# A seventh place for an expert's weights where X was, X kept in the output meanwhile, one buffer for a pair's rows, and the first weights in two loads

## The chip, the cores and the metric

The kernel runs on one core of a Trainium2 chip. Times are device microseconds of one execution. Before the change three runs took 669.09, 669.54 and 670.16 us, so the median is 669.54 us.

The engines of the core: TensorE (PE in the rows; PEld is its weight load), VectorE (DVE), ScalarE (ACT), GpSimd (POOL) and SyncE (SP). SP issues nearly all loads, POOL the indirect gathers and scatters and some stores, ACT the stores of the output. Each engine runs its own list of instructions in order and waits for others at semaphores.

## The reference, cut to what matters

One layer for 640 tokens of 1024 numbers: 512 of a new stream and 8 streams of 16. All is float32.

```
h = RMSNorm(x); z = h @ w_in                       # 3088 columns
x = x + concat(diff_attention(z), gla(z)) @ w_out
h = RMSNorm(x)
group = argmax(h @ w_group); two experts inside the group: top-2 of h @ w_erouter
y = x + sum over the two experts of weight * (silu(h @ w_gate[e]) * (h @ w_up[e])) @ w_down[e]
```

There are 4 groups of 8 experts, so 32 experts. Each has 1024x256 gate, 1024x256 up and 256x1024 down weights: 2048 KB for gate and up together (one load, `egu`) and 1024 KB for down (one load, `edn`). Every expert is loaded whole, 96 MB in all.

## The kernel before, in words

The tokens are 5 tiles of 128. The stages in order: transposes of x and the projection by w_in in six chunks of columns, each in two halves of the inner dimension; linear attention between the chunks; the attention of the prompt; the attention of the streams; w_out and the residual, which leaves its sum in the tile `X` (words 0 to 5K of each partition of a big `arena`); the second norm, the router and tables of which token goes to which slot; then the experts; then the sum.

**The experts.** They run in 16 pairs, 64 slots for each expert, so a pair fills 128 partitions. A pair p takes these steps:

- POOL gathers the pair's rows of the normed input from DRAM into `xs` (line 731). Two buffers. The gather of pair p waits for `xsT_done`: PE must have transposed the rows of pair p-2.
- PE transposes them (line 2225, 8 matmuls), DVE scales them into `xsT` (line 1669), PE multiplies by gate and up (`gate_up`, line 2236, 32 matmuls), ACT and DVE make the hidden values, PE transposes those (line 2244), ACT copies them (line 1066), PE multiplies by down (`down_proj`, line 2256, 16 matmuls).
- ACT copies the two banks to `ysb` (line 1077) and POOL scatters them to DRAM, `ye_dram` (line 719). There are two buffers `ysb`, taken in turn, and ACT waits for the scatter of pair p-2 before it fills one again.

PE's order in the loop is: gate_up(p), down_proj(p-1), transposes of the rows of pair p+1, transposes of the hidden values of pair p. ACT's is: silu(p), `ysb` of pair p-1, hidden values of pair p. POOL's is: gather(p), then scatter(p-4), and so on (`late = 4`).

**The weights.** Six places in the arena (`EPLACE`, `NBUF = 6`) hold an expert each, expert e in place e % 6. The first five load while the stages ahead still run, as soon as each place is free. Place 5 lies on the router's tables and waits for the first two gathers (`gath`, the wait behind line 544). From then on SP loads the gate and up weights of experts 2k+4 and 2k+5 when gate_up of k pairs is done (line 523), and down weights of two experts when down_proj of a pair is done (line 526). All go on one queue, in order.

**The end.** When the last scatter has landed, SP loads the 1280 rows from DRAM in five loads into `yg` (line 586). DVE adds them to `X` with the routing weights (line 1707), and ACT stores the tiles (line 1103). `X` stays in place through all of this.

**The front.** SP loads tile 0 of x, the gains, the first half of the first chunk of weights (`win`, 1024 KB, line 454), then more of x. ACT splits weights into a high part `wH` (line 761), DVE makes the low part `wL` (line 1129), PE transposes tiles of x (line 1720) and multiplies (lines 1734 to 1736).

Of the kernel before, what the change touches and what calls it, by code (L numbers as in the profile page):

```python
# [20 lines left out]
ALU = mybir.AluOpType  # L21
# [3 lines left out]
P = 128  # L25
D = 1024
DC = D // P
# [26 lines left out]
NBUF = 6  # L54
# [18 lines left out]
def build(nc, x, cache_kt, cache_v, state, w_main, w_ga, w_a2b, w_out, cols, k_gain, lam, w_r, b_r,  # L73
          w_gu, w_dn, y_out, k_out, v_out, sp_out, ss_out, hn_dram, ye_dram):
    ctx = ExitStack()
    with ctx:
# [3 lines left out]
        def sem(name):  # L80
            return ctx.enter_context(nc.semaphore(name))
# [137 lines left out]
        EPLACE = [28 * KW, 34 * KW, 40 * KW, 5 * KW, 11 * KW, 17 * KW]  # L219
# [5 lines left out]
        ysb = [at(f"ysb{k}", 23 * KW + k * D, D) for k in range(2)]  # L225
# [4 lines left out]
        YG = [40 * KW, 42 * KW, 44 * KW, 5 * KW, 7 * KW]  # L230
# [66 lines left out]
        ld_small = sem("ld_small")  # L297
        ld_win = [sem(f"ld_win{k}") for k in range(2)]
# [19 lines left out]
        wga_ready = sem("wga_ready")  # L318
# [40 lines left out]
        sp_ready = sem("sp_ready")  # L359
        ss_ready = sem("ss_ready")  # L360
# [8 lines left out]
        vs_ready = sem("vs_ready")  # L369
# [56 lines left out]
        st_y = [sem(f"st_y{k}") for k in range(2)]  # L426
        ysum = sem("ysum")
        st_out = sem("st_out")

# [22 lines left out]
        def _(sp):  # L452
            def w_half(c, k):
                sp.dma_start(win[k][:, :], w_main[c * P:(c + 1) * P, k * HW:(k + 1) * HW]).then_inc(ld_win[k], 16)
# [6 lines left out]
            w_half(0, 0)  # L461
# [38 lines left out]
            sp.wait_ge(ss_ready, 1)  # L500
# [29 lines left out]
            sp.wait_ge(vs_ready, 1)  # L530
# [17 lines left out]

            for k in range(NXS):
                sp.wait_ge(gath[k], 16)  # L550
            gate_up_of(5)
            for e in range(NBUF, NE + 2, 2):
                if e < NE:
                    sp.wait_ge(gu_done, e // 2 - 2)
                    gate_up_of(e)
                    gate_up_of(e + 1)
                if e > NBUF:
                    sp.wait_ge(dn_done, e // 2 - 3)
                    down_of(e - 2)
                down_of(e - 1)  # L560
# [12 lines left out]
            with sp.If(sp.value_load(ovf[0:1, 0:1]) > 0):  # L573
                sp.wait_ge(gu_done, PAIRS)
                sp.wait_ge(dn_done, PAIRS)
                with sp.Fori(1, ROUNDS) as r:
                    with sp.Fori(0, NE // 4) as g:
                        experts(r * 8, g)
                for k in range(2):
                    sp.wait_ge(st_y[k], ROUNDS * (PAIRS // 2) * 16)  # L580

            for k in range(2):
                sp.wait_ge(st_y[k], PAIRS // 2 * 16)
# [9 lines left out]
        def _(pool):  # L593
# [75 lines left out]
            pool.wait_ge(sp_ready, 1)  # L669
            pool.dma_start(sp_out, S).then_inc(st_states, 16)  # L670
            pool.wait_ge(ss_ready, 1)
# [18 lines left out]
            pool.tensor_copy(zVs[:, :], z(C_V, NP)).then_inc(vs_ready, 1)  # L690
# [17 lines left out]
            def pairs(r):  # L708
                first = isinstance(r, int)
                t0 = before(r, 2 * PAIRS, 2 * (PAIRS + 1))  # L710

                def seen():
                    if not first:
                        pool.sem_inc(pool_seen, 1)

                def scatter(p):
                    pool.wait_ge(ysb_ready, r * 2 * PAIRS + 2 * (p + 1))
                    seen()
                    pool.indirect_dma_start(  # L719
                        out=ye_dram, out_offset=bass.IndirectOffsetOnAxis(ap=dst[:, p:p + 1], axis=0),  # L720
                        in_=ysb[p % 2][:, :], in_offset=None, bounds_check=2 * NT * P - 1, oob_is_err=False,
                    ).then_inc(st_y[p % 2], 16)
# [26 lines left out]
        def _(act):  # L749
# [7 lines left out]
            def w_high(c, k):  # L757
                act.wait_ge(ld_win[k], (c + 1) * 16)
                for s in range(4):
                    o = slice(s * 512, (s + 1) * 512)  # L760
                    act.activation(wH[k][:, o], win[k][:, o], ACT.Copy, scale=g1[:, 4 * k + s:4 * k + s + 1]  # L761
                                   ).then_inc(wH_ready, 1)
# [55 lines left out]
            def qT_out(i):  # L818
                act.wait_ge(qT_done, i + 1)
                act.wait_ge(gains_ready, 2)  # L820
                act.activation(qT[:, :, i * P:(i + 1) * P],
                               bank[6 + (NT + i) % 2][:, :].rearrange("p (h t) -> p h t", h=H),
                               ACT.Copy, scale=qg8[:, 0:1]).then_inc(qT_ready, 1)

            for c in range(1, 6):
                for k in range(2):
                    for i in range(NT):
# [52 lines left out]
                        if u == U_QTR:  # L880
                            act.wait_ge(go_done, NT)
                            act.wait_ge(ss_ready, 1)
# [152 lines left out]
            h2_out(0)  # L1035
            std_out(0)
            stream_squares()
            a_high(2)
            h2_out(1)
            std_out(1)  # L1040
# [3 lines left out]
            h2_out(2)  # L1044
            std_out(2)
            a_high(4)
            h2_out(3)
            std_out(3)
            hn_out(2)
            h2_out(4)  # L1050
            std_out(4)
# [36 lines left out]
            with act.If(act.value_load(ovf[0:1, 0:1]) > 0):  # L1088
                with act.Fori(1, ROUNDS) as r:
                    with act.Fori(0, NE // 4) as g:  # L1090
                        for q in range(2):
                            silu(r, 2 * g + q, q)
                            hidden(r, 2 * g + q, q)
                        for q in range(2):
                            act.wait_ge(dn_done, r * PAIRS + 2 * g + q + 1)
                            act.wait_ge(st_y[q], (r * (PAIRS // 2) + g) * 16)
                            for hf in range(2):
                                act.activation(ysb[q][:, hf * 512:(hf + 1) * 512], bank[4 + 2 * q + hf][:, :],
                                               ACT.Copy).then_inc(ysb_ready, 1)
# [7 lines left out]
        def _(dve):  # L1107
# [30 lines left out]
            for i in range(NT):  # L1138
                dve.wait_ge(ld_x[i], 16)
                if i:  # L1140
# [6 lines left out]
                              bc(g1, [P, DC, RANK]), ALU.mult).then_inc(wga_ready, 1)  # L1147
# [64 lines left out]
            def states(i):  # L1212
# [23 lines left out]
                if i == NP - 1:  # L1236
                    dve.nop().then_inc(sp_ready, 1)
# [29 lines left out]
            for c in range(1, 6):  # L1267
                for k in range(2):
                    for i in range(NT):
# [54 lines left out]
                        if u in U_SU:  # L1324
                            stream_states(U_SU.index(u))
                            if u == U_SU[-1]:
                                dve.nop().then_inc(ss_ready, 1)
# [297 lines left out]
            def tables(r):  # L1625
# [11 lines left out]
                else:  # L1637
                    for q in range(2):
                        dve.wait_ge(st_y[q], r * (PAIRS // 2 * 16))
# [62 lines left out]
            for i in range(NT):  # L1702
                dve.wait_ge(ld_x[i], 3 * 16)
# [8 lines left out]
        def _(pe):  # L1712
# [11 lines left out]
            def proj(c, k, i):  # L1724
# [4 lines left out]
                for s in range(DC // 2):  # L1729
# [19 lines left out]
            for i in range(2, NT):  # L1749
                proj(0, 0, i)  # L1750
# [3 lines left out]
            pe.wait_ge(wga_ready, 1)  # L1754
# [310 lines left out]
            def d_pv(b):  # L2065
                pe.wait_ge(d_pt_ready, 2 * b + 2)
                if b == 0:
                    pe.wait_ge(vs_ready, 1)
# [193 lines left out]
            def first_places(p):  # L2262
                return [(2 * p + j) % NBUF for j in range(2)], [2 * p // NBUF + 1] * 2
# [93 lines left out]
```

## Time and profile before

| | us |
|---|---|
| median of 3 runs | 669.54 |
| profiled execution | 669.5 |
| its span in the trace | 667.5 |
| its time outside the span | 2.0 |
| PE busy | 566.3 (85%) |
| DVE busy | 250.8 (38%) |
| ACT busy | 191.8 (29%) |
| POOL busy | 88.7 (13%) |

The profile comes from one execution. Its time, 669.5 us, agrees with the median. The page cuts the span into 40 slices of 16.7 us; the experts fill slices 24 to 39 and the slices before them are bound in turn by PE and by short chains between engines. In the rows, a matmul's busy time is counted whole while matmuls overlap. A DMA has two times: that of its issue on a queue, and the time from its issue to its landing. "DMA share" is the mean over the core's 16 DMA engines.

### The profile page before, as it was taken

What the parts mean: (1) busy time and instruction counts of PE and PEld (TensorE: products, weight loads), DVE (VectorE), ACT (ScalarE), POOL (GpSimd) and SP (SyncE); (2) the same over time, 40 slices, a digit from 0 to 9 for tenths busy, and PEclk for the clock granted to TensorE, in tenths of its full rate; (3) what the DMA queues carried; (4) which work ended last, traced back from release to release, by engine and by line L of the source; (5) the groups of instructions that cost most, each with busy time, mean ns of one, the idle gap of its engine ahead of it and who ended that gap; (6) DMA issues with size and microseconds to landing.
All of it is one profiled execution on the core that took longest, in us unless ns stands there. A gap on an engine that the chain in (4) does not pass through costs nothing.

```text
span 667.5 us, 8610 instructions
## 1 busy us (share of the span) xinstructions
PE 566.3 (85%) x3459; PEld 378.6 (57%) x3459; DVE 250.8 (38%) x536; ACT 191.8 (29%) x439; POOL 88.7 (13%) x125
## 2 busy tenths in 40 slices
PE   4999999999989898978999989999878776868720
PEld 4868787777878676665788873443323332323200
DVE  4733355737548366635434841111101110101006
ACT  4440724322334634438253310111101010101010
POOL 5000000011574200002000210211201111110010
PEclk9999999999999999999999799999978897979875
DMA  8120131121226490058698749999999999999348
GB/s 307 48 92 22 62 145 43 45 64 64 95 88 233 151 425 27 1 190 358 215 424 329 286 131 390 418 424 427 423 428 423 426 426 425 424 426 421 133 163 353
DMA packets 24346, 166.47 MB, mean 249 GB/s; under 512 B 4753, under 2 KB 5329, under 8 KB 11121
## 3 DMA queue, kind: packets, MB, share of 16 engines
q1 hardware_dynamic: 17264, 146.36, 54.8%
q0 software_dynamic: 6320, 16.92, 6.5%
q10 hardware_dynamic: 720, 2.62, 1.0%
q8 instruction: 29, 0.48, 0.3%
q14 instruction: 13, 0.10, 0.0%
HBM read 154.74 MB, written 17.43 MB: 258 GB/s over the span
## 4 chain that ended last, share of the span: by engine, by line
PE 58%; DMA 24%; DVE 6%; ACT 5%; issue 3%; POOL 2%; SPq 1%; POOLq 0%; ACTq 0%; DVEq 0%
DMA egu<-in_w_gu 19%; PE twin L2236 11%; PE twin L1734 7%; PE twin L1736 7%; PE twin L1735 7%; PE twin L2256 4%; PE twin L1993 3%; PE twin L1995 2%; PE twin L1994 2%; DMA yg<-ye_dram 2%; DVE xsT L1669 1%; DMA X<-in_x 1%; PE twin L2074 1%; POOL zK L663 1%; PE twin L1929 1%
## 5 line engine op out<-in xcount | busy, mean ns | idle before, releaser
L2236 PE MATMUL twin<-egu,xsT 128*64 128x512 f32 x512 | 125.4, 646 | 42.0 <-DMA egu<-in_w_gu 35.9
L2236 PEld LDWEIGHTS twin<-egu,xsT 128*64 128x64 f32 x512 | 44.8, 148 | 112.3 <-issue 112.3
L1734 PE MATMUL twin<-wH,hH 128*128 128x512 f32 x240 | 97.1, 404 | 0.0
L1736 PE MATMUL twin<-wH,hL 128*128 128x512 f32 x240 | 93.7, 391 | 0.0
L1735 PE MATMUL twin<-wL,hH 128*128 128x512 f32 x240 | 93.6, 390 | 0.0
L1675 DVE TENSOR_TENSOR hs<-sil,twin 128x256 f32<-128x256 f32 x16 | 6.7, 421 | 163.5 <-ACT sil L1062 163.5
L2256 PE MATMUL twin<-edn,hTs 128*64 128x512 f32 x256 | 58.1, 592 | 1.1 <-ACT hTs L1066 1.1
L1062 ACT ACTIVATE sil<-twin 128x256 f32<-128x256 f32 x16 | 6.1, 383 | 165.8 <-PE twin L2236 165.8
L1734 PEld LDWEIGHTS twin<-wH,hH 128*128 128x128 f32 x240 | 45.1, 188 | 10.6 <-issue 1.8
L1736 PEld LDWEIGHTS twin<-wH,hL 128*128 128x128 f32 x240 | 45.0, 188 | 9.8
L1735 PEld LDWEIGHTS twin<-wL,hH 128*128 128x128 f32 x240 | 45.2, 188 | 8.4
L1129 DVE SCALAR_TENSOR_TENSOR wL<-win,colt,wH 128x512 fp32r<-128x512 f32 x48 | 40.3, 900 | 5.7 <-ACT wH L761 5.7
L2256 PEld LDWEIGHTS twin<-edn,hTs 128*64 128x64 f32 x256 | 21.2, 137 | 34.4 <-issue 33.1
L731 POOL DMA_INDIRECT xs<-hn_dram,idx x16 | 16.1, 1007 | 173.5 <-ACT ysb L1077 151.5
L1669 DVE TENSOR_TENSOR xsT<-twin,colt 128x512 f32<-128x512 f32 x32 | 20.6, 686 | 48.9 <-PE twin L2225 48.9
L761 ACT ACTIVATE wH<-win,colt 128x512 fp32r<-128x512 f32 x48 | 30.7, 716 | 8.8 <-DMA win<-in_w_main 8.8
L1077 ACT ACTIVATE ysb<-twin 128x512 f32<-128x512 f32 x32 | 17.4, 595 | 49.5 <-PE twin L2256 49.5
L898 ACT ACTIVATE E<-twin,nm 128x128 f32<-128x128 f32 (+3 forms) x32 | 16.6, 523 | 30.9 <-DVE nm L1354 30.9
L656 POOL TENSOR_TENSOR zV<-zK 128x512 f32<-128x512 f32 x5 | 5.3, 1052 | 145.0 <-ACT zK L785 145.0
L719 POOL DMA_INDIRECT ye_dram<-ysb,dst x16 | 16.1, 1005 | 55.0 <-ACT ysb L1077 51.3
L2225 PEld LDWEIGHTS twin<-ident,xs 128*128 128x128 f32 x128 | 13.7, 141 | 13.1 <-issue 12.2
L1707 DVE SCALAR_TENSOR_TENSOR X<-yg,wk,X 128x1024 f32<-128x1024 f32 x10 | 12.8, 1285 | 19.9 <-DMA yg<-ye_dram 19.5
(318 smaller groups left out, 837.1 us busy)
## 6 DMA issues: line engine op xcount, KB each, us to landing
egu<-in_w_gu SPq DMA_DIRECT2D x32, 2048.0 KB, 35.2
edn<-in_w_dn SPq DMA_DIRECT2D x32, 1024.0 KB, 39.2
win<-in_w_main SPq DMA_DIRECT2D x12, 1024.0 KB, 5.1
Kc<-in_cache_kt SPq DMA_DIRECT2D x8, 1024.0 KB, 8.2
Vc<-in_cache_v SPq DMA_DIRECT2D x8, 1024.0 KB, 8.7
X<-in_x SPq DMA_DIRECT2D x10, 512.0 KB, 8.1
yg<-ye_dram SPq DMA_DIRECT2D x5, 1024.0 KB, 8.9
woin<-in_w_out SPq DMA_DIRECT2D x3, 1024.0 KB, 5.1
```

The source lines that it names most:

```text
L719: pool.indirect_dma_start(out=ye_dram, out_offset=bass.IndirectOffsetOnAxis(ap=dst[:, p:p + 1], axis=0), in_=ysb[p % 2][:, :], in_offset=N ...
L761: act.activation(wH[k][:, o], win[k][:, o], ACT.Copy, scale=g1[:, 4 * k + s:4 * k + s + 1]).then_inc(wH_ready, 1)
L898: act.activation(E[m % NER][mm][:, 0:L], bank[2 * (m % 2) + mm][:, 0:L], ACT.Exp, bias=nm[:, m % 2, mm:mm + 1], accum_out=es[:, i, h, mm:m ...
L1077: act.activation(ysb[q][:, hf * 512:(hf + 1) * 512], bank[4 + 2 * q + hf][:, :], ACT.Copy).then_inc(ysb_ready, 1)
L1129: dve.scalar_tensor_tensor(out=wL[k][:, o], in0=win[k][:, o], scalar=g1[:, 4 * k + s:4 * k + s + 1], in1=wH[k][:, o].bitcast(F32), op0=ALU ...
L1669: dve.tensor_tensor(xsT[q][:, 4 * hf:4 * hf + 4, :], bank[hf][:, :].rearrange("p (c s) -> p c s", c=4), bc(g2[:, 4 * hf:4 * hf + 4], [P, 4 ...
L1734: pe.matmul(bank[i][:, :], hH[:, d, i, :], wH[k][:, cs], start=(d == 0), stop=False)
L1735: pe.matmul(bank[i][:, :], hH[:, d, i, :], wL[k][:, cs], start=False, stop=False)
L1736: ins = pe.matmul(bank[i][:, :], hL[:, d, i, :], wH[k][:, cs], start=False, stop=(d == DC - 1))
L1993: pe.matmul(out, xH[i % 2][:, c, :], w_high, start=(c == 0), stop=False)
L2236: ins = pe.matmul(bank[2 + q][CAP * j:CAP * j + CAP, :], xsT[q][:, c, j * CAP:(j + 1) * CAP], egu[places[j]][:, c, :], start=(c == 0), sto ...
L2256: ins = pe.matmul(bank[4 + 2 * q + hf][CAP * j:CAP * j + CAP, :], hTs[q][:, f, j * CAP:(j + 1) * CAP], edn[places[j]][:, f, hf * 512:(hf + ...
```

## The change

Seven places for experts. Place 6 is words 0 to 6K, where `X` lies (0 to 5K). So each finished tile of `X` is stored by ACT to `y_out` (`x_store`), and SP loads it back into `X` near the end, when the down_proj of 14 pairs is done and the last weights of place 6 have been used. SP loads the gate and up weights of expert 6 when all five stores have landed, ahead of those of expert 5. Places 3, 4, 5 and the `yg` tiles move by some K words. The down weights of experts 5 and 6 are issued right behind the gate and up weights of expert 5, and the loop runs one expert further ahead. There is one `ysb`, so ACT waits for the scatter of pair p-1 and no longer for that of pair p-2. POOL's `late` is 2 and not 4. At the front the first half chunk of weights is loaded in two pieces, and PE's order has the first two slices of the projection between the transposes of tile 0 and tile 1. Some semaphores are merged.

```diff
-NBUF = 6
+NBUF = 7
-        EPLACE = [28 * KW, 34 * KW, 40 * KW, 5 * KW, 11 * KW, 17 * KW]
+        EPLACE = [28 * KW, 34 * KW, 40 * KW, 6 * KW, 12 * KW, 18 * KW, 0]
-        ysb = [at(f"ysb{k}", 23 * KW + k * D, D) for k in range(2)]
+        ysb = at("ysb", 24 * KW, D)
-        YG = [40 * KW, 42 * KW, 44 * KW, 5 * KW, 7 * KW]
+        YG = [12 * KW + 2 * k * D for k in range(NT)]
...
-            w_half(0, 0)
+            sp.dma_start(win[0][:, 0:HW // 2], w_main[0:P, 0:HW // 2]).then_inc(ld_first, 16)
+            sp.dma_start(win[0][:, HW // 2:HW], w_main[0:P, HW // 2:HW]).then_inc(ld_win[0], 16)
...
+            sp.wait_ge(hn_ready, NP)
+            sp.wait_ge(st_x, NT * 16)
+            gate_up_of(6)
             for k in range(NXS):
                 sp.wait_ge(gath[k], 16)
             gate_up_of(5)
+            down_of(5)
+            down_of(6)
+
             for e in range(NBUF, NE + 2, 2):
                 if e < NE:
-                    sp.wait_ge(gu_done, e // 2 - 2)
+                    sp.wait_ge(gu_done, (e - NBUF) // 2 + 1)
                     gate_up_of(e)
+                if e + 1 < NE:
                     gate_up_of(e + 1)
                 if e > NBUF:
-                    sp.wait_ge(dn_done, e // 2 - 3)
+                    sp.wait_ge(dn_done, (e - NBUF) // 2)
                     down_of(e - 2)
-                down_of(e - 1)
+                    if e - 1 < NE:
+                        down_of(e - 1)
+            sp.wait_ge(dn_done, PAIRS - 2)
+            for i in range(NT):
+                sp.dma_start(X[:, i, :], y_out[i]).then_inc(ld_x[i], 16)
...
-                late = 4 if first else 3
+                late = 2 if first else 3
...
+            def x_store(i):
+                act.wait_ge(x2_ready, 2 * NT + 2 * i + 2)
+                act.dma_start(y_out[i], X[:, i, :]).then_inc(st_x, 16)
...
-                else:
-                    act.wait_ge(st_y[q], (r * (PAIRS // 2) + p // 2) * 16)
+                if p:
+                    act.wait_ge(st_y, (r * PAIRS + p) * 16)
                 for hf in range(2):
-                    act.activation(ysb[q][:, hf * 512:(hf + 1) * 512], bank[4 + 2 * q + hf][:, :],
+                    act.activation(ysb[:, hf * 512:(hf + 1) * 512], bank[4 + 2 * q + hf][:, :],
...
             for i in range(NT):
-                dve.wait_ge(ld_x[i], 3 * 16)
+                dve.wait_ge(ld_x[i], 4 * 16)
...
-            for i in range(3):
-                x_tr(i)
-            proj(0, 0, 0)
+            x_tr(0)
+            proj(0, 0, 0, (0, 1))
+            x_tr(1)
+            proj(0, 0, 0, (2, 3))
+            x_tr(2)
+            proj(0, 0, 1)
             x_tr(3)
-            proj(0, 0, 1)
+            proj(0, 0, 2)
             x_tr(4)
```

GpSimd's instructions from the first gather on, before the change; `xs<-hn_dram,idx` is a gather, `ye_dram<-ysb,dst` a scatter:

```order
L731 DMA xs<-hn_dram,idx 128x1024 [waits xs_zero,idx_ready,st_hn1,st_hn0]
L731 DMA xs<-hn_dram,idx 128x1024
L731 DMA xs<-hn_dram,idx 128x1024 [waits xsT_done] x3
L719 DMA ye_dram<-ysb,dst 1280x1024 [waits ysb_ready]
L731 DMA xs<-hn_dram,idx 128x1024 [waits xsT_done]
L719 DMA ye_dram<-ysb,dst 1280x1024 [waits ysb_ready]
```

The same place after the change:

```order
L740 DMA xs<-hn_dram,idx 128x1024 [waits xs_zero,idx_ready,st_hn1,st_hn0]
L740 DMA xs<-hn_dram,idx 128x1024
L740 DMA xs<-hn_dram,idx 128x1024 [waits xsT_done]
L728 DMA ye_dram<-ysb,dst 1280x1024 [waits ysb_ready]
L740 DMA xs<-hn_dram,idx 128x1024 [waits xsT_done]
L728 DMA ye_dram<-ysb,dst 1280x1024 [waits ysb_ready]
```

The first scatter now stands behind three gathers and not behind five, so the gathers of pairs 3 and later stand behind the scatter of the pair three before them.

SyncE's loads around the start of the experts, before the change; `egu` is gate and up, `edn` is down:

```order
L526 DMA edn<-in_w_dn 128x2048 [waits ssq1,out_done]
L523 DMA egu<-in_w_gu 128x4096
L526 DMA edn<-in_w_dn 128x2048
L523 DMA egu<-in_w_gu 128x4096 [waits gath1,gath0]
L523 DMA egu<-in_w_gu 128x4096 [waits gu_done]
L523 DMA egu<-in_w_gu 128x4096
L526 DMA edn<-in_w_dn 128x2048
```

The same place after the change:

```order
L526 DMA edn<-in_w_dn 128x2048 [waits ssq1,out_done]
L523 DMA egu<-in_w_gu 128x4096
L526 DMA edn<-in_w_dn 128x2048
L523 DMA egu<-in_w_gu 128x4096 [waits st_x,hn_ready]
L523 DMA egu<-in_w_gu 128x4096 [waits gath1,gath0]
L526 DMA edn<-in_w_dn 128x2048 x2
L523 DMA egu<-in_w_gu 128x4096 [waits gu_done]
L523 DMA egu<-in_w_gu 128x4096
```

One load of 2048 KB has moved ahead of the wait for the gathers, and two of 1024 KB ahead of the first wait for gate_up.

## Rows read from the trace of the kernel before

**Rows 1.** The page's chain that ended last, by line.
```profile
DMA egu<-in_w_gu 19%; PE twin L2236 11%; PE twin L1734 7%; PE twin L1736 7%; PE twin L1735 7%; PE twin L2256 4%; PE twin L1993 3%; PE twin L1995 2%; PE twin L1994 2%; DMA yg<-ye_dram 2%; DVE xsT L1669 1%; DMA X<-in_x 1%; PE twin L2074 1%; POOL zK L663 1%; PE twin L1929 1%
```
**Rows 2.** Windows: stretch, its us, busy by engine, TensorE clock, DMA share, GB/s.
```profile
390.00:400.00 10.00, 8.14 (x63) 6.46 (x64) 2.78 (x13) 1.71 (x3) 3.10 (x3) 1.00 0.40 104
410.00:420.00 10.00, 9.18 (x48) 4.07 (x46) 1.71 (x3) 1.85 (x4) 0.65 (x1) 1.00 1.02 431
620.00:630.00 10.00, 7.87 (x30) 2.84 (x32) 0.00 (x0) 0.00 (x0) 0.00 (x0) 0.83 0.33 138
```
**Rows 3.** Timeline of PE's gate_up: start, us, instruction, idle before it.
```profile
397.73 7.09 PE L2236 MATMUL twin<-egu,xsT 128*64 128x512 f32 x32 [1.11 <-DVE xsT L1669]
...
432.20 7.09 PE L2236 MATMUL twin<-egu,xsT 128*64 128x512 f32 x32 [0.82 <-DVE xsT L1669]
...
487.56 9.39 PE L2236 MATMUL twin<-egu,xsT 128*64 128x512 f32 x32 [5.85 <-DMA egu<-in_w_gu]
504.67 8.78 PE L2236 MATMUL twin<-egu,xsT 128*64 128x512 f32 x32 [3.05 <-DMA egu<-in_w_gu]
...
538.45 7.09 PE L2236 MATMUL twin<-egu,xsT 128*64 128x512 f32 x32 [3.15 <-DMA egu<-in_w_gu]
...
622.13 8.67 PE L2236 MATMUL twin<-egu,xsT 128*64 128x512 f32 x32 [4.16 <-DMA egu<-in_w_gu]
```
**Rows 4.** DMA issues between 404.9 and 405.2: KB each, us to landing.
```profile
egu<-in_w_gu SPq DMA_DIRECT2D x1, 2048.0 KB, 9.2
```
**Rows 5.** Timeline of GpSimd's gathers and scatters, near the start and the end.
```profile
406.62 0.99 POOL L731 DMA_INDIRECT xs<-hn_dram,idx  x1 [8.23 <-PE twin L2225]
419.36 0.99 POOL L731 DMA_INDIRECT xs<-hn_dram,idx  x1 [11.75 <-ACT ysb L1077]
420.65 1.02 POOL L719 DMA_INDIRECT ye_dram<-ysb,dst  x1 [0.30 <-issue]
...
636.13 0.97 POOL L719 DMA_INDIRECT ye_dram<-ysb,dst  x1 [16.51 <-ACT ysb L1077]
641.25 0.97 POOL L719 DMA_INDIRECT ye_dram<-ysb,dst  x1 [4.14 <-ACT ysb L1077]
```
**Rows 6.** Timeline of copies to ysb, and of one pair's transposes and gate_up.
```profile
430.18 1.08 ACT L1077 ACTIVATE ysb<-twin 128x512 f32<-128x512 f32 x2 [3.05 <-PE twin L2256]
442.65 1.09 PE L2225 MATMUL twin<-ident,xs 128*128 128x128 f32 x8
444.78 2.79 PE L2236 MATMUL twin<-egu,xsT 128*64 128x512 f32 x12 [0.82 <-DVE xsT L1669]
639.39 1.08 ACT L1077 ACTIVATE ysb<-twin 128x512 f32<-128x512 f32 x2 [3.75 <-PE twin L2256]
```
**Rows 7.** The page's DMA issues: median us to landing of gathers and scatters.
```profile
xs<-hn_dram,idx POOLq DMA_INDIRECT x16, 10.5
ye_dram<-ysb,dst POOLq DMA_INDIRECT x16, 14.2
```
**Rows 8.** Landings one by one: gather at 391.3; scatters at 604.6 and 636.1.
```profile
xs<-hn_dram,idx POOLq DMA_INDIRECT x1, 4.2
ye_dram<-ysb,dst POOLq DMA_INDIRECT x1, 11.7
ye_dram<-ysb,dst POOLq DMA_INDIRECT x1, 4.3
```
**Rows 9.** Timeline of the front, SP's issue, ACT, PE.
```profile
1.73 0.42 SPq L454 DMA_DIRECT2D win<-in_w_main  x1
9.86 2.56 ACT L761 ACTIVATE wH<-win,colt 128x512 fp32r<-128x512 f32 x4 [2.81 <-DMA win<-in_w_main]
11.08 3.55 PE L1720 MATMUL twin<-ident,X 128*128 128x128 f32 x16 [4.68 <-DMA X<-in_x]
14.39 0.48 PE L1734 MATMUL twin<-wH,hH 128*128 128x512 f32 x1
17.21 1.04 PE L1720 MATMUL twin<-ident,X 128*128 128x128 f32 x8
```

More of the change, by code:

```diff
@@ L297, in build @@
         ld_small = sem("ld_small")
+        ld_first = sem("ld_first")
         ld_win = [sem(f"ld_win{k}") for k in range(2)]
@@ L317, in build @@
         gains_ready = sem("gains_ready")
-        wga_ready = sem("wga_ready")
         ga_done = sem("ga_done")
@@ L358, in build @@
         silu_ready = sem("silu_ready")
-        sp_ready = sem("sp_ready")
-        ss_ready = sem("ss_ready")
+        states_ready = sem("states_ready")
         st_states = sem("st_states")
@@ L368, in build @@
         att_zero = sem("att_zero")
-        vs_ready = sem("vs_ready")
         s_done = sem("s_done")
@@ L425, in build @@
         ysb_ready = sem("ysb_ready")
-        st_y = [sem(f"st_y{k}") for k in range(2)]
+        st_y = sem("st_y")
         ysum = sem("ysum")
         st_out = sem("st_out")
+        st_x = sem("st_x")
         items = [(i, h) for i in range(NP) for h in range(H)]
@@ L499, in _ @@
             sp.wait_ge(go_done, NT)
-            sp.wait_ge(ss_ready, 1)
+            sp.wait_ge(states_ready, 2)
             sp.wait_ge(st_states, 2 * 16)
@@ L529, in _ @@
             sp.wait_ge(d_s_done, NB)
-            sp.wait_ge(vs_ready, 1)
+            sp.wait_ge(att_zero, 4)
             sp.wait_ge(o_done, NI)
@@ L578, in _ @@
                         experts(r * 8, g)
[L579 to L583, printed above, removed]
+                sp.wait_ge(st_y, ROUNDS * PAIRS * 16)
+            sp.wait_ge(st_y, PAIRS * 16)
             sp.wait_ge(dn_done, PAIRS)
@@ L667, in _ @@
             squares(C_Q, 1)
-            pool.wait_ge(sp_ready, 1)
+            pool.wait_ge(states_ready, 1)
             pool.dma_start(sp_out, S).then_inc(st_states, 16)
-            pool.wait_ge(ss_ready, 1)
+            pool.wait_ge(states_ready, 2)
             pool.dma_start(ss_out, S0).then_inc(st_states, 16)
@@ L688, in _ @@
             pool.memset(Cb[:, :, :], 0.0).then_inc(att_zero, 1)
-            pool.tensor_copy(zVs[:, :], z(C_V, NP)).then_inc(vs_ready, 1)
+            pool.tensor_copy(zVs[:, :], z(C_V, NP)).then_inc(att_zero, 1)
             pool.wait_ge(ro_ready, 2)
@@ L720, in scatter @@
                         out=ye_dram, out_offset=bass.IndirectOffsetOnAxis(ap=dst[:, p:p + 1], axis=0),
-                        in_=ysb[p % 2][:, :], in_offset=None, bounds_check=2 * NT * P - 1, oob_is_err=False,
-                    ).then_inc(st_y[p % 2], 16)
-                late = 4 if first else 3
+                        in_=ysb[:, :], in_offset=None, bounds_check=2 * NT * P - 1, oob_is_err=False,
+                    ).then_inc(st_y, 16)
+                late = 2 if first else 3
                 pool.wait_ge(idx_ready, r + 1)
@@ L757, in w_high @@
             def w_high(c, k):
-                act.wait_ge(ld_win[k], (c + 1) * 16)
+                first = c == 0 and k == 0
+                act.wait_ge(ld_first if first else ld_win[k], 16 if first else (c + 1) * 16)
                 for s in range(4):
+                    if first and s == 2:
+                        act.wait_ge(ld_win[0], 16)
                     o = slice(s * 512, (s + 1) * 512)
@@ L819, in qT_out @@
                 act.wait_ge(qT_done, i + 1)
-                act.wait_ge(gains_ready, 2)
+                act.wait_ge(gains_ready, 3)
                 act.activation(qT[:, :, i * P:(i + 1) * P],
@@ L881, in _ @@
                             act.wait_ge(go_done, NT)
-                            act.wait_ge(ss_ready, 1)
+                            act.wait_ge(states_ready, 2)
                         if U_QTR <= u < U_QTR + NT:
@@ L1035, in _ @@
             h2_out(0)
+            x_store(0)
             std_out(0)
@@ L1039, in _ @@
             h2_out(1)
+            x_store(1)
             std_out(1)
@@ L1044, in _ @@
             h2_out(2)
+            x_store(2)
             std_out(2)
@@ L1047, in _ @@
             h2_out(3)
+            x_store(3)
             std_out(3)
@@ L1050, in _ @@
             h2_out(4)
+            x_store(4)
             std_out(4)
@@ L1095, in _ @@
                             act.wait_ge(dn_done, r * PAIRS + 2 * g + q + 1)
-                            act.wait_ge(st_y[q], (r * (PAIRS // 2) + g) * 16)
+                            act.wait_ge(st_y, (r * PAIRS + 2 * g + q) * 16)
                             for hf in range(2):
-                                act.activation(ysb[q][:, hf * 512:(hf + 1) * 512], bank[4 + 2 * q + hf][:, :],
+                                act.activation(ysb[:, hf * 512:(hf + 1) * 512], bank[4 + 2 * q + hf][:, :],
                                                ACT.Copy).then_inc(ysb_ready, 1)
@@ L1236, in states @@
                 if i == NP - 1:
-                    dve.nop().then_inc(sp_ready, 1)
+                    dve.nop().then_inc(states_ready, 1)
             def go_out(i):
@@ L1326, in _ @@
                             if u == U_SU[-1]:
-                                dve.nop().then_inc(ss_ready, 1)
+                                dve.nop().then_inc(states_ready, 1)
                         if 27 <= u < 27 + NT:
@@ L1637, in tables @@
                 else:
-                    for q in range(2):
-                        dve.wait_ge(st_y[q], r * (PAIRS // 2 * 16))
+                    dve.wait_ge(st_y, r * (PAIRS * 16))
                     tstep(1, dve.tensor_scalar(rmask, rn[:, :, :], cur[:, 0:1], None, ALU.is_equal))
@@ L1722, in x_tr, with proj @@
                     ins.then_inc(xT_done, 1)
-            def proj(c, k, i):
+            def proj(c, k, i, slices=(0, 1, 2, 3)):
                 if c == 0:
@@ L1728, in proj @@
                     pe.wait_ge(z_free, NT * (c - 1) + i + 1)
-                for s in range(DC // 2):
+                for s in slices:
                     if i == 0:
@@ L1742, in _ @@
             pe.wait_ge(id_ready, 1)
-            for i in range(3):
-                x_tr(i)
-            proj(0, 0, 0)
+            x_tr(0)
[4 more added lines that the diff above has]
+            proj(0, 0, 1)
             x_tr(3)
-            proj(0, 0, 1)
+            proj(0, 0, 2)
             x_tr(4)
-            for i in range(2, NT):
+            for i in range(3, NT):
                 proj(0, 0, i)
@@ L1752, in _ @@
                 proj(0, 1, i)
-            pe.wait_ge(wga_ready, 1)
+            pe.wait_ge(gains_ready, 2)
             for a in range(2):
@@ L2067, in d_pv @@
                 if b == 0:
-                    pe.wait_ge(vs_ready, 1)
+                    pe.wait_ge(att_zero, 4)
                 pe.wait_ge(ld_v[b % NKV], 16 * (b // NKV + 1))
@@ L2262, in first_places @@
             def first_places(p):
-                return [(2 * p + j) % NBUF for j in range(2)], [2 * p // NBUF + 1] * 2
+                return [(2 * p + j) % NBUF for j in range(2)], [(2 * p + j) // NBUF + 1 for j in range(2)]
             xs_tr(0, 0, 0, 0)
```

2 lines of the change are left out of this document (1 added, 1 removed).

## The prediction

> **What bounds the kernel now.** First the chain that ended last: a fifth of the span is the landing of `egu`, the gate and up weights, and no other wait is near it [rows 1]. Then the windows, for the stretch in which that holds. The DMA engines are at 0.40 just before the experts start, full at 1.02 behind it, and at 0.33 in the last stretch that has weights [rows 2]. Then PE's timeline of gate_up. Before, it starts every 12.58 us (432.20 in rows 3, the next at 444.78 in rows 6) and waits only for `xsT`; from 487.56 on it waits for weights each time [rows 3, 6]. From 487.56 (pair 7) to 622.13 (pair 15) are 8 pairs in 134.6 us, so 16.8 us a pair. The reader is to see two lines, PE's from 397.7 with 12.6 us a pair and the weights' with 16.8, which cross at pair 7. Only the later counts for the start of the last gate_up, T15 = 622.13. What follows it to the end of the span is 45.4 us. So I work out how far T15 moves, how far the start of the experts moves, and how the 45.4 us change.
>
> **Front.** PE starts its first product at 14.39, behind three tiles' transposes, since the whole half chunk landed only for the ACT copy at 9.86 [rows 9]. After the change two of its four slices can run in PE's idle 4.68 us ahead of 11.08, and the other two behind tile 1. At 14.4 PE then has done one product (14.39 to 17.21, 2.8 us) and lacks one tile's transposes (1.04 at full clock, 1.8 in the first ones): 1.0 to 1.8 us gained. Bounds: nothing, if the first piece lands as late as the whole did, and 2.8, the whole product. I take -1.4. The extra load's issue on SP, 0.42 us as the one at 1.73, delays tile 1 of x and is inside that. The stages up to 390 us hand it on, since their chains start from PE.
>
> **Start of the experts.** ACT issues five more DMAs, at 0.42 us each if ACT takes as long as SP for one [rows 9], 2.1 us in all. ACT waits for PE's products between its steps there, so I count them as hidden, and 0.4 if one is not. The stores are 2.6 MB and expert 6's gate and up weights 2.1 MB, together 4.7 MB and some 11 us at the 431 GB/s of the full stretch, in a stretch where the engines have idle time (0.40 in rows 2). The first gather took 4.2 us there [rows 8]; in the full stretch gathers take 10.5 [rows 7]. The weights' load ends about when it starts, so it costs between 0 and 1.5 us; I take +0.6.
>
> **The weights' line.** It gains the gate and up weights of expert 6, which no longer load in the full stretch: 2.1 MB at 431 GB/s, 4.9 us. It gains a pause too: the next load of that kind was issued at 405 on a queue nearly empty and took 9.2 us for 4.9 us of bytes [rows 4], and now two down loads stand there; I take 1.5 of the 4.3. But in the new order one more down load, 1.05 MB or 2.4 us, stands ahead of the gate and up weights of an odd expert 2p+1: batches now begin with that expert, behind down weights up to 2p-2, where before the batch of both stood behind 2p-3. Sum: -4.9 - 1.5 + 2.4 = -4.0, T15 = 618.1. Were this all, the kernel would be faster.
>
> **PE's line gets a loop through the DMA queue.** This is the step the change is decided by. POOL issued gather(3) at 406.62, right behind the transposes of pair 1 [rows 5]. Now it stands behind scatter(0), which needs `ysb` of pair 0. That copy of 1.08 us [rows 6] ends 12.58 us ahead of the one at 430.18, at 418.7. From a copy's end to its scatter are 0.8 us (639.39 + 1.08 to 641.25) and from one indirect DMA to the next 1.3 (419.36, 420.65) [rows 5, 6]. So gather(3) goes out at 420.8 and not 406.6. A gather landed 10.5 us after its issue and the scatter 1.3 us behind it 14.2 us after its own [rows 7]. Two in a row on one queue, so the gather, now second, should take what the scatter took: 14.2, and with 10.5 to 16 as bounds. It lands at 435.0, its transposes were due at 430.1 (12.58 ahead of 442.65), and from transposes to gate_up are 2.1 us (442.65, 444.78): T3 = 437.1, not 432.20.
>
> From there it repeats. Gather(p+1) is behind scatter(p-2), and down_proj(p-2) follows gate_up(p-1). From T(p-1): 10.5 to the end of down_proj(p-2), 1.1 for the copy, 0.8, 1.3, the landing, 2.1. So T(p+1) = T(p-1) + 15.8 + 14.2 = 30.0 us for two pairs, where PE needs 25.2 and the weights 33.6. Six such cycles from T3 give T15 = 437.1 + 180 = 617.1, beside 618.1 of the weights. In themselves the two lines meet. But in each cycle PE now stands still for 3.4 to 4.8 us in front of a transpose. Idle times of 5.85 and 3.05 us were followed by a gate_up of 9.39 and 8.78 us, one of 3.15 by 7.09 [rows 3]: the granted clock fell to 1.2 GHz for part of it in two of these three. That is 1.7 to 2.3 us, and here it lies inside the cycle. At half of the cycles with 2.0 us, six cycles give +6, T15 = 623.1; the last cycle has a shorter landing, since the queue empties (11.7 for the scatter at 604.6 [rows 8]), for which I take 0.5 off: 622.6, or +0.5 against before. The cover that is gone is two pairs of lead; what it costs has 617 and 631 as ends (no fall of the clock; landing 14.2 with a fall in every cycle).
>
> The Trainium skill, DMA: Bandwidth & Descriptors, section Anatomy of one DMA, fits a POOL DMA by 2.0 us plus its bytes at 436 GB/s, so 3.2 us for 512 KB. The trace agrees with that only where the queues are empty, 4.2 and 4.3 us in rows 8. By the rule the cycle would be 15.8 + 3.2 = 19.0 us, under PE's own 25.2, and the weights' line would decide, the first rival.
>
> **The one ysb.** ACT waits for the scatter of the pair before. Scatter to scatter: 11.7 landing [rows 8], 1.1 copy, 0.8, so 13.6 us a pair, under the 15 of the loop: hidden. At the end it shows. The scatter at 636.13 takes 4.3 us, lands at 640.4, and the last copy that began at 639.39 begins at 640.5 [rows 5, 6, 8]: +1.1. Bounds 0 and 3, the latter if the reload of X is still in the queue. That reload is 2.6 MB, issued when the DMA share was 0.33 [rows 2], done some 10 us ahead of the `yg` loads: nothing.
>
> **Sum.** -1.4 front, +0.6 start, +0.5 at T15, +1.1 end: +0.8. The profiled execution took 669.5 us (span 667.5, 2.0 around it) and agrees with the median of 669.54, so 670.3 us. Less than 0.2%, 1.3 us, is what a measurement of this kernel cannot tell from no change.
>
> **Rivals.**
> The weights' line alone decides (gathers land early enough, or the clock stays up and the landing is at most 14): -1.4 + 0.6 - 4.0 + 1.1 = -3.7, 665.8 us. For it: at 14.2 us and no fall the loop gives 617.1. Against it: every stall is over 3 us.
> The loop with a fall of the clock in every cycle: T15 is 437.1 + 6 x 32.0 = 629.1, less 1.5 for the last landings, +5.5 against before; with the rest 675.3 us, slower. It decides as soon as a stalled pair's cycle is over 30.5 us. For it: 5.85 and 3.05 us both brought a fall. Against it: 3.15 did not, and where a stalled pair is late the other parity is not.
> The early load of expert 6 does not happen early, because the stores land behind the gathers: the pause stays full, the line gains nothing, some 670 to 672.
>
> **How the numbers follow.** The loop and the weights nearly meet, as forecast: 0.40, itself 667 to 673, so about 0.10 faster, 0.15 same, 0.15 slower. Weights alone: 0.35, faster but for 0.02. Clock in every cycle: 0.20, slower. Expert 6 late: 0.05, slower or same. Faster 0.43, same 0.18, slower 0.39. The range leaves out 1 in 10 on each side: 664.3 to 676.
>
> **What would show it.** Front: first product ahead of 11 us. Loop: the third gather's successor issued at about 420 and the gate_up of pair 3 at 437 behind a wait of PE's transposes for the gather; idle time ahead of the transposes in every second pair and fewer waits for `egu`. If gate_up still waits for `egu` from pair 7 on and the transposes wait for nothing, the first rival holds. DMA share at 390 to 400 should rise from 0.40. I am wrong if a second indirect DMA lands in 10 us or less in the full stretch, or if the start of the experts moves by more than 2 us.

## The result

| | median us | runs | ratio to before, 95% interval |
|---|---|---|---|
| before, in the same series | 671.01 | 8 | |
| after | 676.36 | 8 | 1.0091 [1.0069, 1.0113] |

The change makes the kernel slower by 0.9%, some 6 us. (The two medians alone are 5.35 us or 0.8% apart, which lies in the interval.) In the experiments each ratio is to runs of the kernel before in the same series, whose median was 669.45 to 670.03 us, so ratios are compared there and not medians. The profiled execution of the changed kernel has a span of 676.6 us, against 667.5. It took 678.5 us, the longest of the eight and 2.1 over their median, while the profiled one of before, 669.5, lies under its median. So the 9.1 us between the two traces are more than the change costs in the median.

### The profile page after: what moved, and what is told of

The parts are those of the page before. It is cut to its first block, busy times and chain, and to the rows that moved or that the text cites. A ratio compares the mean times of both kernels' runs of the same rounds, so it can differ in the third digit from the quotient of the medians.

```text
span 676.6 us, 8624 instructions
## 1 busy us (share of the span) xinstructions
PE 572.3 (85%) x3459; PEld 383.1 (57%) x3459; DVE 251.5 (37%) x536; ACT 191.6 (28%) x439; POOL 88.8 (13%) x125
## 4 chain that ended last, share of the span: by engine, by line
PE 61%; DMA 19%; DVE 6%; ACT 6%; issue 4%; POOL 3%; SPq 0%; POOLq 0%; ACTq 0%; DVEq 0%
DMA xs<-hn_dram,idx 14%; PE twin L2259 12%; PE twin L1754 7%; PE twin L1756 7%; PE twin L1755 7%; PE twin L2279 5%; PE twin L2016 3%; PE twin L2018 2%; PE twin L2017 2%; DMA yg<-ye_dram 2%; PE twin L2248 2%; DVE xsT L1689 1%; PE twin L2097 1%; DMA ye_dram<-ysb,dst 1%; ACT ysb L1098 1%
## 5 line engine op out<-in xcount | busy, mean ns | idle before, releaser
L2259 PE MATMUL twin<-egu,xsT 128*64 128x512 f32 x512 | 123.1, 636 | 11.0 <-DVE xsT L1689 11.0
L2259 PEld LDWEIGHTS twin<-egu,xsT 128*64 128x64 f32 x512 | 43.4, 147 | 81.6 <-issue 81.6
L1754 PEld LDWEIGHTS twin<-wH,hH 128*128 128x128 f32 x240 | 45.4, 189 | 14.6 <-issue 5.7
L2248 PE MATMUL twin<-ident,xs 128*128 128x128 f32 x128 | 23.6, 344 | 34.6 <-DMA xs<-hn_dram,idx 34.6
L1756 PEld LDWEIGHTS twin<-wH,hL 128*128 128x128 f32 x240 | 45.4, 189 | 9.9
L2248 PEld LDWEIGHTS twin<-ident,xs 128*128 128x128 f32 x128 | 18.6, 176 | 47.5 <-DMA xs<-hn_dram,idx 41.0
```

Of the source, the lines that this page charges most:

```text
L1754: pe.matmul(bank[i][:, :], hH[:, d, i, :], wH[k][:, cs], start=(d == 0), stop=False)
L1756: ins = pe.matmul(bank[i][:, :], hL[:, d, i, :], wH[k][:, cs], start=False, stop=(d == DC - 1))
L2248: ins = pe.transpose(bank[hf][:, c * P:(c + 1) * P], xs[q][:, (4 * hf + c) * P:(4 * hf + c + 1) * P], ident[:, :])
L2259: ins = pe.matmul(bank[2 + q][CAP * j:CAP * j + CAP, :], xsT[q][:, c, j * CAP:(j + 1) * CAP], egu[places[j]][:, c, :], start=(c == 0), sto ...
```

## The profile after

First the chain of the page, by line, of the changed kernel ([rows 1] is the same line of before):

```profile
DMA xs<-hn_dram,idx 14%; PE twin L2259 12%; PE twin L1754 7%; PE twin L1756 7%; PE twin L1755 7%; PE twin L2279 5%; PE twin L2016 3%; PE twin L2018 2%; PE twin L2017 2%; DMA yg<-ye_dram 2%; PE twin L2248 2%; DVE xsT L1689 1%; PE twin L2097 1%; DMA ye_dram<-ysb,dst 1%; ACT ysb L1098 1%
```

`egu`, a fifth of the span in [rows 1], is gone from the line. The gathers (`xs<-hn_dram,idx`) stand in its place with 14%. The waits of PE and of its weight load say the same (engine, line, waited for: us in total, times, longest):

```profile
PEld twin L2248 <- DMA xs<-hn_dram,idx: 41.0, 8, 7.3
PE twin L2248 <- DMA xs<-hn_dram,idx: 34.6, 8, 6.4
```

L2248 is the transposes of a pair's rows. The two waits lie beside each other: at 502.5 us PE's weight load had waited 7.29 us and PE 6.41, and both went on together. So PE stood still for 34.6 us and not for the sum. PE's timeline of gate_up (line 2259), cut, answers to [rows 3]. It has pairs 0 to 3, then 5, 7, 8, 9, 11 and 13 to 15:

```profile
398.93 9.06 PE L2259 MATMUL twin<-egu,xsT 128*64 128x512 f32 x32 [0.88 <-DVE xsT L1689]
410.22 7.09 PE L2259 MATMUL twin<-egu,xsT 128*64 128x512 f32 x32 [0.85 <-DVE xsT L1689]
422.79 7.09 PE L2259 MATMUL twin<-egu,xsT 128*64 128x512 f32 x32 [0.82 <-DVE xsT L1689]
439.81 7.41 PE L2259 MATMUL twin<-egu,xsT 128*64 128x512 f32 x32 [0.45 <-DVE xsT L1689]
...
471.51 8.62 PE L2259 MATMUL twin<-egu,xsT 128*64 128x512 f32 x32 [0.45 <-DVE xsT L1689]
...
505.39 8.74 PE L2259 MATMUL twin<-egu,xsT 128*64 128x512 f32 x32 [0.45 <-DVE xsT L1689]
519.63 7.09 PE L2259 MATMUL twin<-egu,xsT 128*64 128x512 f32 x32 [0.82 <-DVE xsT L1689]
538.96 9.02 PE L2259 MATMUL twin<-egu,xsT 128*64 128x512 f32 x32 [0.45 <-DVE xsT L1689]
...
572.60 7.57 PE L2259 MATMUL twin<-egu,xsT 128*64 128x512 f32 x32 [0.45 <-DVE xsT L1689]
...
604.07 8.89 PE L2259 MATMUL twin<-egu,xsT 128*64 128x512 f32 x32 [0.45 <-DVE xsT L1689]
618.46 7.09 PE L2259 MATMUL twin<-egu,xsT 128*64 128x512 f32 x32 [0.82 <-DVE xsT L1689]
631.03 7.09 PE L2259 MATMUL twin<-egu,xsT 128*64 128x512 f32 x32 [0.82 <-DVE xsT L1689]
```

None waits for weights any more. The start of pair 15 has moved from 622.13 to 631.03, 8.9 us of the 9.1 us by which the span grew; what follows it is 45.6 us and was 45.4. One cycle of two pairs, from the gate_up of pair 7 to that of pair 9, can be read off the timeline from 502 to 539 us:

```profile
502.55 1.97 PE L2248 MATMUL twin<-ident,xs 128*128 128x128 f32 x8 [6.41 <-DMA xs<-hn_dram,idx]
...
513.95 3.61 PE L2279 MATMUL twin<-edn,hTs 128*64 128x512 f32 x16
517.50 1.10 PE L2248 MATMUL twin<-ident,xs 128*128 128x128 f32 x8
517.60 1.09 ACT L1098 ACTIVATE ysb<-twin 128x512 f32<-128x512 f32 x2 [3.05 <-PE twin L2279]
...
519.48 1.01 POOL L728 DMA_INDIRECT ye_dram<-ysb,dst  x1 [18.89 <-ACT ysb L1098]
...
520.80 1.00 POOL L740 DMA_INDIRECT xs<-hn_dram,idx  x1 [0.31 <-issue]
...
536.12 1.97 PE L2248 MATMUL twin<-ident,xs 128*128 128x128 f32 x8 [5.97 <-DMA xs<-hn_dram,idx]
```

The gather issued at 520.80 took, in the page's view of DMA issues for that moment alone:

```profile
xs<-hn_dram,idx POOLq DMA_INDIRECT x1, 15.3
```

From 505.39 the steps are 8.6 us of gate_up, 3.5 of down_proj, 1.2 to the end of the copy, 0.8 to the scatter, 1.3 to the gather, 15.3 to its landing and 2.8 to the next gate_up, 33.5 in all; 538.96 - 505.39 is 33.6. The DMA engines stay full all the while, and TensorE's granted clock is 0.63 of its full 2.4 GHz in this stretch, so part of it ran at 1.2 GHz (columns as in rows 2):

```profile
530.00:540.00 10.00, 3.58 (x16) 2.47 (x16) 1.38 (x2) 1.47 (x3) 2.01 (x2) 0.63 1.02 429
```

## The experiments

**The order on GpSimd's queue.** Theory A: the gather behind the scatter closes the loop. Theory B: the single ysb does. Theory C: the traffic of X does. The first run issues each scatter one gather later:

```diff
-                late = 2 if first else 3
+                late = 3
```

> The changed kernel with GpSimd's scatters one place later in its order (late = 3 and not 2): gather(p+1) then stands behind scatter(p-3) and not scatter(p-2), so it is issued a whole pair earlier, and the scatters still go out as soon as their rows are there. Theory A, the order on GpSimd's queue closes a loop of two pairs through a gather that lands 15 us after issue: the transposes' waits for gathers (75 us over 16 pairs for PE and its weight load, 6 us in each second pair) go, gate_up waits for egu again from pair 6 to 8 on, the last gate_up starts at 616 to 619 and not 631, and the kernel takes 664 to 668 us, under the kernel before. Theory B, the single ysb, each copy waiting for the scatter of the pair before, makes it slow: stays at 674 to 678. Theory C, the traffic of the stores and the reload of X takes it: stays at 674 to 678.

Measured: 666.63 us, 0.9951 [0.9923, 0.998] to before. PE's timeline from pair 7 on:

```profile
486.89 7.09 PE L2259 MATMUL twin<-egu,xsT 128*64 128x512 f32 x32 [0.82 <-DVE xsT L1689]
503.49 8.46 PE L2259 MATMUL twin<-egu,xsT 128*64 128x512 f32 x32 [3.86 <-DMA egu<-in_w_gu]
```

PE waits for weights again, and pairs 3 to 7 follow each other at 12.58 us. The last gate_up began at 620.97 in this execution, 1.97 us above the range expected. The experts had begun late in it, at 400.40. The next run has GpSimd's old order:

```diff
-                late = 2 if first else 3
+                late = 4 if first else 3
```

> The changed kernel with late = 4, GpSimd's order of before, with the one ysb kept. Each scatter goes out behind a gather, with 14 us to land, and the copy of the next pair waits for it: 14.2 + 2 us, so 16.2 a pair against 16.8 of the weights. Theory A: faster than the change, 668 to 673, slower than with late = 3. Theory B (the single ysb is the cause): this is the worst form, 678 or more. Theory C: 674 to 678.

Measured: 666.22 us, 0.9945 [0.9924, 0.9966], 1.8 us under the range expected. It was expected slower than late = 3 and is the same within the intervals. ACT waits long for scatters here, but the ratio shows no cost of it beside late = 3, while PE waits for weights (a line of its page, with ACT's idle time and its releaser last):

```profile
L1098 ACT ACTIVATE ysb<-twin 128x512 f32<-128x512 f32 x32 | 17.4, 594 | 100.3 <-DMA ye_dram<-ysb,dst 89.3
```

The last gate_up began at 618.06. From late = 2 to 4 the ratio falls from 1.0091 to 0.9945, 1.5% or 9.8 us. Then the other way about, late = 2 alone in the kernel before:

```diff
-                late = 4 if first else 3
+                late = 2 if first else 3
```

> The kernel before with late = 2 and nothing else: six places, two ysb, X stays in place. Theory A: the loop of two pairs at 33 to 34 us is there too, and it gives a last gate_up at 629 to 634, a time 4 to 9 us over before, 675 to 680. Theories B and C: within 1 us of before.

Measured: 676.40 us, 1.0104 [1.006, 1.0147]. Six places, two ysb, X untouched, and the same waits of PE for the gathers:

```profile
PE twin L2225 <- DMA xs<-hn_dram,idx: 35.5, 8, 6.2
```

Its last gate_up began at 630.68, in the range of theory A. B and C cannot make this run slow, since it has neither, so theory A stands. With this order alone the kernel is as slow as with the whole change, within the intervals.

**The clock inside the loop.** The edit gives PE 20 matmuls of the identity to do, ahead of the transposes that wait. Their results are not used, and the trace has two records for each.

```diff
+                if p % 2 == 0 and 2 <= p < PAIRS - 2:
+                    for j in range(20):
+                        pe.matmul(bank[0][:, 0:P], ident[:, :], ident[:, :], start=True, stop=True)
```

> The changed kernel with 20 matmuls of the identity into a free bank ahead of each stalled set of transposes (pairs 3, 5 to 13), results unused, so that PE is not idle there and its clock stays at 2.4 GHz. Theory A with the clock's fall inside the loop: each cycle of two pairs falls from 33.6 us to 31 to 32, five or six times 1.5 to 2.5 us, 666 to 670 us. If the clock's fall is not inside the loop (the gather's landing alone sets it), no gain, 675 to 678.

Measured: 672.23 us, 1.0047 [1.0021, 1.0074]; 0.44% or 2.9 us under the change, a third to a half of what was expected. The timeline of pair 7, one of those that stalled:

```profile
495.01 4.73 PE L2295 MATMUL twin<-ident 128*128 128x128 f32 x40
500.34 1.09 PE L2248 MATMUL twin<-ident,xs 128*128 128x128 f32 x8 [0.59 <-DMA xs<-hn_dram,idx]
...
502.46 7.09 PE L2259 MATMUL twin<-egu,xsT 128*64 128x512 f32 x32 [0.82 <-DVE xsT L1689]
```

The granted clock is 1.00 from 500 to 510 us here and was 0.56 in the change. At the full clock the transposes take 1.09 us and not 1.97 and gate_up 7.09 and not 8.7; all six pairs that stalled in the change (3, 5 and on to 13) have a gate_up of 7.09 us here. From pair 7 to pair 13 the kernel takes 93.2 us, where the change took 98.7: 1.8 us a cycle, as expected. In the profiled execution the last gate_up began at 623.34, 7.7 us earlier than in the change; its span of 667.9 is well under the median of the runs, so the span is no measure of the effect here, and why the median gains less is open. Three things in the trace take some of the gain back. The even pairs now wait for their gathers too, 0.63 to 1.98 us in pairs 4 to 12. The 20 matmuls have a fixed length of 4.73 us: the gather of pair 11 landed at 561.8, and its transposes began at 563.20, when the matmuls were done. And the gate_up of pair 4, at 450.52, took 9.98 us; no added matmuls stand ahead of an even pair.

**What the other parts are worth.** The front alone in the kernel before (cut; the edit is that of the change's diff, both loads and PE's order):

```diff
-            w_half(0, 0)
+            sp.dma_start(win[0][:, 0:HW // 2], w_main[0:P, 0:HW // 2]).then_inc(ld_first, 16)
+            sp.dma_start(win[0][:, HW // 2:HW], w_main[0:P, HW // 2:HW]).then_inc(ld_win[0], 16)
...
+            x_tr(0)
+            proj(0, 0, 0, (0, 1))
+            x_tr(1)
+            proj(0, 0, 0, (2, 3))
```

> The kernel before with the front of the change alone: the first half chunk of weights in two loads and two slices of the first product between the transposes of tiles 0 and 1. By the prediction 1.4 us faster (0 to 2.8), and by the first gathers' issue in the traces (390.2 and 390.0 with the change's front, 391.3 and 391.9 without) 1.1 to 1.9, so a ratio of 0.9980 with a spread of 0.002. A rival, that the gain is used up before the experts: no difference.

Measured: 668.49 us, 0.9972 [0.9945, 1.0], 1.9 us; zero is at the interval's edge. Its trace does not bear out the reading of the first gathers: here the first one went out at 392.57, later than the 391.26 of before. In the traces with the new front it goes out anywhere from 389.38 to 393.43, so one trace cannot show a gain of 1 to 2 us.

The next run takes the seventh place out of the change, with late = 4 (cut):

```diff
-NBUF = 7
+NBUF = 6
...
-            sp.wait_ge(st_x, NT * 16)
-            gate_up_of(6)
...
-            x_store(0)
```

> The change without its seventh place: six places, X stays in SBUF, no stores and reloads of it, the one ysb and the front kept, late = 4. Against the run with seven places and late = 4 it measures the seventh place; against front_only, the single ysb. By the weights' line: the seventh place is worth 4.0 us less 1.0 to 1.7 us for the slower first gather, so this one takes 668.5 to 670. Rival: the seventh place is worth nothing once the order is right, 666 to 667.

Measured: 670.29 us, 1.0000 [0.9979, 1.0022]. Against seven places and late = 4 (0.9945) the seventh place is worth 0.55% or 3.7 us; against front_only (0.9972) the single ysb costs 0.28% or 1.9 us, a difference within the intervals. With late = 2 the seventh place gains nothing that can be seen (1.0091 for the change, 1.0104 for the kernel before with late = 2).

Then seven places and late = 4, with expert 6 loaded later:

```diff
-            gate_up_of(6)
             for k in range(NXS):
                 sp.wait_ge(gath[k], 16)
+            gate_up_of(6)
```

> Seven places, late = 4, but the gate and up weights of expert 6 are issued behind the wait for the first two gathers and no longer ahead of it. The first gather should land after 4.2 to 4.5 us and not 5.7, the experts start 1.0 to 1.7 us earlier, and the weights' line is 4.9 us later for the bytes: 3 to 4 us slower than with the early load, 669 to 671. Rival, that the early load only moves traffic into the gather's way: no slower, 665 to 667.

Measured: 669.31 us, 0.9995 [0.997, 1.0021], so the early load is worth 0.5% or 3.4 us. By these ratios nearly all that the seventh place brings is the load of expert 6 in the idle stretch; that the deeper buffering brings little more (1.0000 to 0.9995) is known only to some 0.3%. The first gather landed in 4.1 us here and in 5.6 with the early load.

**The end.** The last two copies of the rows and the scatter between them, with late = 4, and ahead of them the last two gate_ups:

```profile
602.17 7.09 PE L2259 MATMUL twin<-egu,xsT 128*64 128x512 f32 x32 [2.32 <-DMA egu<-in_w_gu]
618.06 8.66 PE L2259 MATMUL twin<-egu,xsT 128*64 128x512 f32 x32 [2.30 <-DMA egu<-in_w_gu]
...
630.19 1.08 ACT L1098 ACTIVATE ysb<-twin 128x512 f32<-128x512 f32 x2 [3.05 <-PE twin L2279]
632.05 0.98 POOL L728 DMA_INDIRECT ye_dram<-ysb,dst  x1 [14.64 <-ACT ysb L1098]
636.62 1.08 ACT L1098 ACTIVATE ysb<-twin 128x512 f32<-128x512 f32 x2 [5.07 <-DMA ye_dram<-ysb,dst]
```

The second copy waits for the scatter; it starts 6.43 us behind the first, where 5.12 lay between them with two ysb (634.27 in that trace to 639.39 in [rows 6]). The next edit, with late = 4, gives PE matmuls to do while the last gate_up waits for its weights:

```diff
+                if p == PAIRS - 1:
+                    pe.wait_ge(hTs_ready, p - 1)
+                    for j in range(14):
+                        pe.matmul(bank[2 + p % 2][:, 0:P], ident[:, :], ident[:, :], start=True, stop=True)
```

> Seven places, late = 4, and 14 matmuls of the identity ahead of the last gate_up, results unused, in the time in which PE waits for its weights. In the run without them the last gate_up took 8.66 us at a clock that had fallen, and nothing follows it that hides it: 1.6 us faster, 664.6, if the clock then stays up; 0 to 1 us slower if the matmuls outlast the wait of about 3 us or the clock falls anyway.

Measured: 666.89 us, 0.9957 [0.9932, 0.9981], no gain over 0.9945. The last gate_up took 7.09 us, but the 14 matmuls took 3.29 us where the wait in late4 was 2.30. Then a second buffer for the last pair only, with late = 4 (cut):

```diff
+        ysb_last = at("ysb_last", 23 * KW, D)
...
-                if p:
+                last = p == PAIRS - 1
+                if p and not last:
```

> Seven places, late = 4, and the last pair's rows copied to a second buffer in a place whose expert is done, so that the last copy need not wait for the scatter of pair 14. In the traces the two last copies start 5.1 us apart with two ysb and 6.2 to 6.4 with one: 1.1 to 1.3 us faster than late = 4 alone, a ratio near 0.992 to 0.993 to the kernel before. Rival: the last scatters run beside each other and land later, no gain.

Measured: 664.52 us, 0.9928 [0.9906, 0.9949], 1.1 us under late4, the size expected though the intervals overlap. The last run adds 8 matmuls in the wait of the last gate_up (cut):

```diff
...
+                    for j in range(8):
+                        pe.matmul(bank[2 + p % 2][:, 0:P], ident[:, :], ident[:, :], start=True, stop=True)
```

> The same with 8 matmuls of the identity ahead of the last gate_up and not 14, so that they end inside its wait of 2.3 us (14 took 3.3 us). If the clock stays up, the last gate_up takes 7.1 us and not 8.7, up to 1.6 us faster than tail_ysb; if the idle time that is left lets it fall all the same, no difference.

Measured: 663.34 us, 0.991 [0.9888, 0.9931], the fastest of all. Its end, with 8 matmuls in the wait for weights:

```profile
614.18 1.95 PE L2295 MATMUL twin<-ident 128*128 128x128 f32 x16
...
616.66 7.09 PE L2261 MATMUL twin<-egu,xsT 128*64 128x512 f32 x32 [0.53 <-issue]
...
627.22 1.09 ACT L1100 ACTIVATE ysb<-twin 128x512 f32<-128x512 f32 x2 [3.05 <-PE twin L2281]
629.08 0.97 POOL L729 DMA_INDIRECT ye_dram<-ysb,dst  x1 [13.09 <-ACT ysb L1100]
632.33 1.08 ACT L1100 ACTIVATE ysb_last<-twin 128x512 f32<-128x512 f32 x2 [3.75 <-PE twin L2281]
```

The copies are 5.11 us apart again, and gate_up takes 7.09 us. That the matmuls add to tail_ysb (0.9928 to 0.991) is not clear of the intervals, and the 7.09 us of one execution do not show that they held the clock: late4 has two waits of 2.3 us without matmuls, one with a gate_up of 7.09 us behind it and one with 8.66, and in this execution too the pair before waited 2.31 us and took 7.09.

## Why the prediction was wrong

The loop was foreseen and its price was too low: 670.3 us and "same" were forecast, and the slower rival, the loop with a fall of the clock in every cycle, came out, at 675.3 forecast and 676.36 measured. That the two are so near is in part luck. The rival put the last gate_up at 627.6; in the trace it began at 631.03, in an execution 2.1 us over the median.

- **The step that failed** is in the sum of the loop: "At half of the cycles with 2.0 us, six cycles give +6". The clock fell in all six stalled pairs, 3 to 13, whose transposes had waited 3.7 to 6.4 us, since the loop brings the stall back at the same place in each cycle. The first five cycles took 31.7, 33.9, 33.6, 33.6 and 31.5 us, 164.3 in all, where the forecast has 155 (30.0 each and 5 for the clock). The slower clock cost 5.9 us in their gate_ups and, which the sum left out, 0.8 us a cycle from landing to gate_up, for the transposes were counted at the full clock: 9.9 us and not 5.
- **The landing.** The gathers of pairs 5 to 13 that close the cycles landed after 14.3 to 15.7 us, 4.0 us more over the five than the 14.2 taken. The median in [rows 7] held four scatters of the emptying queue (11.7, 8.0, 4.3 and 3.2 us).
- **The last cycle** took 27.0 us and not 30.5. Its gather landed in 7.1 us and pair 15 waited for nothing; the forecast took 0.5 us off for that. This hides 3.5 us of the miss.
- **The start of the loop.** Gather(3) went out at 424.01 (forecast 420.8) and landed in 12.9 us; the gate_up of pair 3 began at 439.81, 2.7 us after its forecast. The forecast for front and start together was -0.8, but the gate_up of pair 0 began at 398.93, 1.2 us later than before: the first gather went out 1.1 us earlier and landed in 5.9 us and not 4.2 [rows 8]. It also took 9.06 us with its clock fallen, which the prediction had no term for, and so pair 0's rows came 3.2 us later than before. With it the miss at pair 15 adds up: 2.7 + 9.3 - 3.5 = 8.5, and 631.03 is 8.4 us over the 622.6 forecast.
- **Whether the weights set the pace.** Three of the cycles lie at the 33.6 us that the weights take for two pairs. But no gate_up waits for weights, and in `warm` two cycles took 31.3 and 31.6 us with the DMA engines as full. So the loop alone sets the time.
- **Front, -1.4.** Measured alone -1.9, at the edge of what shows. The first product began at 9.84 us, ahead of 11 as expected.
- **The weights' line, -4.0.** The seventh place is worth 3.7 us by the ratios. The last gate_up of late4 began at 618.06, forecast 618.1. That agreement is partly luck, since 618.1 is without the front and the start (617.3 with them), and single executions of seven places and late = 3 or 4 with the early load of expert 6 have it from 616.38 to 620.97.
- **The rule of the Trainium skill** (DMA: Bandwidth & Descriptors, Anatomy of one DMA) gives an estimate of 3.2 us for a gather, and with it the first rival. The trace does not agree with it in the full stretch, 15.3 us. It agrees for the last scatter alone, 3.2 us; the one before took 4.5, and the 4.2 and 4.3 of [rows 8] are 1 us over the rule too.
- **The end, +1.1.** The last two copies are 1.3 us further apart with late = 4, and in the changed kernel, where they start at 641.59 and 648.04, 6.45 apart. Yet there the stretch behind the start of the last gate_up grew by 0.2 us only, since that gate_up took 7.09 us where it took 8.67 before. The reload of X cost nothing that the rows show.
- **The chances.** The slower rival had 0.20. Its condition, a cycle over 30.5 us, was met by the forecast's own average of 31. The three rows read had two falls. The whole trace of before has nine gate_ups that waited for weights: behind 3.71, 4.16, 5.59, 5.66 and 5.85 us each took 8.67 us or more, behind 2.31, 2.44, 3.05 and 3.15 only one of four did. With stalls of 3.4 to 4.8 us forecast, that supported every cycle better than half of them.

## What to carry to other kernels

Where an engine's queue issues both the input and the output of a pipeline, the order between them is a dependence: an input behind an output that waits for compute makes a loop whose length holds the DMA's full landing time. Take that landing from the loaded stretch and from the place in its queue. A stall that a loop repeats can repeat its clock penalty too, six times of six here, so count it in each cycle, and in all the work behind the stall.

## What the runs showed of the hardware that was not expected

An indirect gather of 128 rows of 4 KB landed in 4.2 us where the DMA share was 0.40, and in 15.3 behind a scatter while weights streamed at 429 GB/s, although it moves at most 0.5 MB. In the full stretch the place in the queue told more than the direction: before the change the gathers went first and landed in 8.6 to 12.0 us, the scatters 1.3 us behind them in 11.4 to 16.8; in the changed kernel eight scatters that went first (422.68 to 532.07) landed in 10.1 to 11.4 us, and the gathers of pairs 3 to 13 behind their scatters in 12.9 to 15.7.

With matmuls of an identity in the wait of PE, all six pairs that had stalled took 7.09 us for gate_up, at a granted clock of 1.00 where it was read (500 to 510 us), and not 7.4 to 9.0.
